# A two-layer diffusion trunk in split fp32: weight splits leave GpSimd, the last hidden group goes by token halves, one modulation block moves into the mixer

## The reference

```python
def swiglu(h, wg, wu, wd):
    return (jax.nn.silu(h @ wg) * (h @ wu)) @ wd

def ffn_sublayer(s, m, i, g, wg, wu, wd):
    h = modulate(rmsnorm(s, g), m[3 * i], m[3 * i + 1])
    return s + 0.5 * m[3 * i + 2] * swiglu(h, wg, wu, wd)

def hybrid_layer(x, ctx, mod_x, mod_c, p, lam_init, rope, need_ctx_out):
    x, ctx = ffn_sublayer(x, ...), ffn_sublayer(ctx, ...)
    h = modulate(rmsnorm(x, p['g_mix']), mx[3], mx[4])
    ...
    y = concat([a_lat, conv_lat, four_lat]) @ p['w_out']   # attention, convolution, Fourier
    x = x + mx[5] * y                                      # and the same for ctx in layer 0
    x, ctx = ffn_sublayer(x, ...), ffn_sublayer(ctx, ...)
```

## Time and profile before

| what | us |
|---|---|
| runs: median, lowest, highest | 2766.89, 2766.89, 2768.28 |
| profiled execution, and its span | 2764.62, 2762.8 |
| TensorE matmul busy | 2614.2 (95% of the span) |
| VectorE busy | 1979.2 (72%) |
| ScalarE busy | 958.2 (35%) |
| GpSimd busy | 197.9 (7%) |
| TensorE's mean granted clock, of full speed | 0.979 |

### The profile page before, as it was taken

One profiled execution on the slowest core, in us unless ns is written; L12 is line 12 of the kernel. 1 busy time (PEld: TensorE's weight loads), 2 busy tenths in 40 slices (PEclk: granted clock), 3 DMA queues, 4 the chain that ended last, 5 costly groups with the idle time before them and its releaser, 6 DMA issues.

```text
span 2762.8 us, 40297 instructions
## 1 busy us (share of the span) xinstructions
PE 2614.2 (95%) x14704; PEld 2368.5 (86%) x14704; DVE 1979.2 (72%) x3130; ACT 958.2 (35%) x1674; POOL 197.9 (7%) x324
## 2 busy tenths in 40 slices
PE   6999999979987999999998999999999988899998
PEld 4899999968955879999998799999988846788886
DVE  5688888888837377888887877777758665544445
ACT  4333333323147333332332434333423264322222
POOL 2000000030003210000001100000020013100001
PEclk8999999989999999999999999999999999999999
DMA  8134333331101113323333133334313110222221
GB/s 297 54 109 132 117 100 106 119 110 61 64 31 46 31 54 93 118 93 125 106 115 117 44 103 115 104 106 125 118 41 97 62 61 31 77 92 91 91 91 61
DMA packets 190672, 256.21 MB, mean 93 GB/s; under 512 B 7262, under 2 KB 130764, under 8 KB 190540
## 3 DMA queue, kind: packets, MB, share of 16 engines
q1 hardware_dynamic: 190540, 254.43, 29.1%
HBM read 252.31 MB, written 2.10 MB: 92 GB/s over the span
## 4 chain that ended last, share of the span: by engine, by line
PE 84%; DVE 8%; ACT 3%; issue 2%; DMA 1%; POOL 1%; DVEq 0%; ACTq 0%; SPq 0%; POOLq 0%
PE ps L1182 26%; PE ps L1184 25%; PE ps L1183 25%; PE ps L1628 1%; PE ps L1652 1%; PE ps L1573 1%; DVE h_lo L2241 1%; DVE nb L2862 1%; PE ps L1640 1%; DVE tn L2230 1%; DVE rstd L2220 1%; ACT e L2095 1%; POOL sqsum L1174 1%; DVE w_lo L2214 1%; DMA raw<-in_w_ffn_down 1%
## 5 line engine op out<-in xcount | busy, mean ns | idle before, releaser
L1182 PE MATMUL ps<-h_hi,w_hi 128*128 128x384 f32 (+2 forms) x2440 | 845.0, 346 | 26.8 <-DVE h_lo L2241 18.5
L1184 PE MATMUL ps<-h_hi,w_lo 128*128 128x384 f32 (+2 forms) x2440 | 838.9, 344 | 0.0
L1183 PE MATMUL ps<-h_lo,w_hi 128*128 128x384 f32 (+2 forms) x2328 | 802.8, 345 | 0.0
L1182 PEld LDWEIGHTS ps<-h_hi,w_hi 128*128 128x128 f32 x2440 | 465.3, 191 | 69.8 <-issue 23.4
L1184 PEld LDWEIGHTS ps<-h_hi,w_lo 128*128 128x128 f32 x2440 | 465.1, 191 | 31.8
L1183 PEld LDWEIGHTS ps<-h_lo,w_hi 128*128 128x128 f32 x2328 | 444.1, 191 | 30.6 <-issue 1.5
L1731 ACT ACTIVATE w_hi<-raw 128x512 fp32r<-128x512 f32 x348 | 210.1, 626 | 351.1 <-PE ps L1184 271.9
L1182 PE MATMUL ps<-t_hi,w_hi 128*128 128x384 f32 x864 | 294.3, 341 | 0.0
L1184 PE MATMUL ps<-t_hi,w_lo 128*128 128x384 f32 x864 | 293.6, 340 | 0.0
L1183 PE MATMUL ps<-t_lo,w_hi 128*128 128x384 f32 x864 | 293.4, 340 | 0.0
L2302 DVE SCALAR_TENSOR_TENSOR side_acc<-side_raw,ccol,side_acc 128x512 f32<-128x512 f32 x364 | 257.9, 744 | 4.2 <-DMA side_raw<-in_w_ada 3.9
(11 more groups left out here) (210 smaller groups left out, 3660.6 us busy)
## 6 DMA issues: line engine op xcount, KB each, us to landing
side_raw<-in_w_ada SPq DMA_DIRECT2D x240, 256.0 KB, 2.7
raw<-in_w_ffn_gate SPq DMA_DIRECT2D x44, 1024.0 KB, 5.3
raw<-in_w_ffn_up SPq DMA_DIRECT2D x44, 1024.0 KB, 5.3
raw<-in_w_ffn_down SPq DMA_DIRECT2D x44, 1024.0 KB, 5.0
raw<-in_w_in SPq DMA_DIRECT2D x14, 1024.0 KB, 5.3
ada_buf<-in_w_ada SPq DMA_DIRECT2D x12, 1024.0 KB, 12.6
raw<-in_w_out SPq DMA_DIRECT2D x8, 1024.0 KB, 5.2
raw<-in_w_in SPq DMA_DIRECT2D x8, 512.0 KB, 7.1
```

Source lines behind the costliest of these rows:

```text
L1182: mm(out, wh, xh, start=start, stop=False, skip_group_check=reopened)
L1183: mm(out, wh, xl, start=False, stop=False, skip_group_check=reopened)
L1184: return mm(out, wl, xh, start=False, stop=stop, skip_group_check=reopened)
```

## The change

It has five parts.

- GpSimd splits no weight tile; `POOL_SPLITS` is gone and VectorE does those eight. At the end of an FFN of `FAST` ScalarE and VectorE split the first of the next two tiles ahead of the last group's product, and the second after two residual adds of the second piece. At the end of a mixer VectorE splits `U` behind its last residual add.
- The last group's hidden tile is finished by token halves: the right half (`right_slots`, ScalarE's high half, `hid_low_half(x, 1)`), for which the down product's first piece waits, then the left (`left_slots`, `hid_low_half(x, 0)`), for which the second piece waits.
- The side product of group 9 comes after the fifth of the last seven products (`LAST_EVENT = 4`), and shift and scale of the next norm are made ahead of the last product, not between the residual adds and the reciprocal.
- The modulation block of group 10 in FFN 0 (block 16 of layer 0) moves into the first mixer: its loads behind a small table's, its sixteen sums behind the convolution taps, its side product behind the first attention scores.
- The first piece's `stat` comes after the second tile (j == 1) of the second piece at the ends of FFNs 0 to 2. The second piece's comes after the second k step of the first up product (all gate products ahead of it) in FFNs 1 to 3, and at k == 3 in the mixer's projection.

```diff
-FIRST_EVENT, SECOND_EVENT, LAST_EVENT = 4, 4, 1
+FIRST_EVENT, SECOND_EVENT, LAST_EVENT = 4, 4, 4
+MIX_SIDE = (0, NG - 1)
+STAT_AT = (None, 1, 1, 1)
...
-POOL_SPLITS = {1: (("K", 0, 0), ("K", 0, 1)), 2: (("U", 1, 0),), 3: (("G", 2, 0), ("U", 2, 0)),
-               4: (("K", 1, 0), ("K", 1, 1)), 5: (("U", 3, 0),)}
...
@@ the sync engine's queue, mixer @@
+                if key == ("S", 0):
+                    side(*MIX_SIDE, range(KD))
...
@@ GpSimd @@
-                for key in POOL_SPLITS.get(q, ()):
-                    if q % 3 != 2:
-                        split(key)
                 for s, j in square_order(q):
-                    if q % 3 == 2 and (s, j) == (seg_order(q)[1], 6):
-                        for key in POOL_SPLITS[q]:
-                            split(key)
...
@@ TensorE @@
-                                if k == 2 and s == first and ws == "g" and q:
+                                if k == STAT_AT[f] and s == first and ws == "u":
                                     stat(q, second)
...
-                pe.wait_ge(hid_ready, hid_number(f, g))
                 first, second = last_slots(f)
                 for s in (first, second):
                     o, n = PIECES[s][:2]
+                    pe.wait_ge(hid_ready, hid_number(f, g, 0 if f in FAST and s == first else 1))
...
-                        if s == second and j == 3:
+                        if s == second and j == (1 if f in FAST else 3):
                             stat(after, seg_order(after)[0])
-                    if s == first:
-                        side(lambda x: x, NG - 1)
...
-                        if s == 1 and k == 2:
+                        if s == 1 and k == 3:
                             stat(q, 0)
...
+                    if (l, i) == (0, 0):
+                        side_product(MIX_SIDE[0], lambda x: x, MIX_SIDE[1])
...
@@ ScalarE @@
                 for j in range(KD):
                     square(q, first, j)
+                if f in FAST:
+                    split(nxt[1])
+                    for j in range(2):
+                        square(q, second, j)
+                    root(q, first)
...
@@ VectorE @@
                         middle("U", x)
-                        side_end(q)
-                        side(x, (0, 1))
-                        corner("U", x)
-                        side(x, (2, 3))
-                        first_block(x)
-                        right_block(x)
-                        side(x, (4, 5))
-                        lower_blocks(x)
-                        hid_low(x)
-                        side(x, (6, 7))
+                        corner("U", x)
+                        if SIDE_GROUPS[f]:
+                            dve.wait_ge(side_done, side_number((f, p)) + 1)
+                        shift_scale((1, 3, 4)[f] // 3, (1, 3, 4)[f] % 3)
+                        split(nxt[0])
+                        first_block(x)
+                        right_slots(x)
+                        side_end(q)
+                        hid_low_half(x, 1)
+                        left_slots(x)
+                        hid_low_half(x, 0)
                         return
...
+                if f in FAST:
+                    for j in range(2):
+                        add_one(j, second)
+                    split(nxt[1])
+                    add_one(2, second)
+                    last_seg = second
+                    first, second = seg_order(q)
+                    over_rms(q, first)
...
+                if l == MIX_SIDE[0]:
+                    side_rows(*MIX_SIDE, range(KD))
...
                     add_out(2 * v + 1, s)
+                    if (v, s) == (3, second):
+                        split(("U", 2 * l + 1, 0))
```

192 lines of the change are left out of this document (107 added, 85 removed).

## The result

The changed kernel takes 2736.81 us (median of four runs, 2733.11 to 2741.49), the kernel before 2766.89 us (four runs, 2765.81 to 2768.28). The ratio is 0.9886, with a 95% interval from 0.9873 to 0.9899: 30 us less. The forecast was 2726, with a range from 2717 to 2740. The profiled execution took 2733.11 us with a span of 2731.3, so 31.5 us less than that of before.

A forecast was written before the change was run, and what follows sets the result against it. TensorE was taken as the bound, losing time only in waits and lower clock at five seams; gains of 41.6 us less 0.6 gave 41 us off the profiled 2764.62, 2723.6, plus 2.3 for the median: 2726, range 2717 to 2740.

The forecast's parts named there:

- (a): Rival: VectorE becomes the bound at the seams through held reciprocals and late GpSimd additions; 10 to 13 us return, 2737; chance 0.15.
- (b): Rival: the gain at the second and third FFN's starts is lost again as VectorE bounds their first groups; 2733; chance 0.11.
- One sign that the prediction had named for being wrong: New TensorE waits inside the FFNs' first groups; the other sign was waits for VectorE growing by more than 10 us.
- The held VectorE instruction: At the seams between sublayers, a GpSimd split of 4.60 us holds VectorE about 4.06 us; VectorE's own split takes 2.28.
- 8 x (4.06 - 2.28) = 14 us: VectorE's gain from taking back eight GpSimd splits, each said to hold it 4.06 us against 2.28 for its own.
- Seam 1: First FFN's end to first mixer: the mixer's second piece starts at 609.9 instead of 624.57, 14.7 us gained.
- Seams 2 and 5: Ends of the first and second mixer, into the second and last FFN: 5.6 and 10.1 us gained.
- Seam 3: Second FFN's end to third FFN: the second piece starts at 1541.2 instead of 1551.16, 10.0 us gained.
- Seam 4: Third FFN's end to second mixer: only the token halves and the order act, 1.2 us gained.
- less 0.6 for the second pieces at seams 2 and 3: Deduction of 0.6 us at the second and third FFN's starts, where second pieces follow VectorE's low halves step by step.
- unpriced by any row: A reciprocal beside a GpSimd addition: taken as 0, or held up to 1.3 us at each of three seams.
- (c): Rival: the side block's loads and sums in the mixer delay VectorE's mean subtraction; slower than before, 2774; chance 0.03.

The follow-up runs named there:

- pool_back: The changed kernel with the eight weight splits on GpSimd again: 2741.47 us, ratio 0.9911 to the kernel before.
- before_dve_splits: The kernel before with only the eight weight splits moved from GpSimd to VectorE: 2760.65 us, ratio 0.9979 to the kernel before.
- stat_bank_j2: stat_bank with the first piece's sum of squares asked for after the second piece's third tile at the ends of FFNs 0 to 2: 2726.98 us.
- best_a: stat_bank with the second piece's sum of squares asked for earlier, during the first gate products, in FFNs 1 and 2: 2726.59 us, ratio 0.9854.
- stat_old: The changed kernel with the sums of squares over the partitions asked for in their old places: 2744.16 us, ratio 0.9910 to the kernel before.
- stat_bank: The changed kernel with the second piece's sum of squares in the PSUM bank that the ninth product will use: 2730.09 us, ratio 0.9868.
- second execution: The changed kernel itself profiled once more, nothing altered; its second set of runs had a median of 2739.30 us.
- halves_off: The changed kernel with the last group's product, high and low halves made whole again, not by token halves: 2740.49 us, ratio 0.9895.

## Why the prediction was right, and where it was not

**Forecast and result.** Faster was right, and the time lay within the range, though near its upper end: 2736.81 us in the first set of runs and 2739.30 in the second, where the range ends at 2740. The gain was 30 us by the medians and 31.5 in the profiled executions, against 41. The range had room for this loss because of rivals (a) and (b), and neither of them was its cause. One sign that the prediction had named for being wrong did come: new waits inside the FFNs' first groups, of 1.10, 1.07 and 2.28 us.

**The held VectorE instruction** was read rightly: 4.56 us beside GpSimd's split, 0.56 without. The choice of this row against the notion that offloading helps a busy VectorE is borne out by pool_back (5 us slower) and before_dve_splits (6 us faster than before). The two pages quoted there don't stand against each other, either: the Trainium skill ("Perfetto Trace Analysis", section "Optimizing Scalar/DVE Operations") goes on in its next sentence that GpSimd and VectorE share an SBUF read port, so that moving work between them might not help. But "8 x (4.06 - 2.28) = 14 us" was too much. Only five of the eight splits held a VectorE instruction, since the residual adds beside the other three read PSUM: the row for it was in the trace. The other three only add their 2.28 us to VectorE, so in VectorE's time the price is 5 x 4.06 less 8 x 2.28, which is 2 us. The 14 us were no term of the forecast's sum, which went seam by seam; there the runs show 6 us for the splits moved alone, and steps of 7 us when they are put back.

**Seam 1.** "The down product starts at 573.3": 572.69. "587.5" for the reciprocal: 586.50. "22.4" from there to the second piece's first low half: 608.06 + 0.75 - 586.50 = 22.3. The wait before the down product was 1.5 us, not 3.0, mostly since shift and scale took 0.26 + 0.24 us, not 0.87 + 1.38: in the rows of before, single instructions of 0.78 and 1.30 us stand beside GpSimd's additions, where they take 0.17 otherwise. Behind this short wait the clock stayed up (1.00 from 572 to 610 us), and the eight tiles took 5.9 us, not the 7.4 that the forecast had for a partly lower clock. "The sum of squares, asked for two tiles earlier, isn't late" was wrong: TensorE waited for it for 1.64, 1.65 and 1.72 us at seams 1, 3 and 4. stat_bank_j2 shows that this cost nothing, because VectorE sets the end of these seams.

**Seams 2 and 5** came out as the forecast had them, 5.6 for 5.6 and 10.0 for 10.1.

**Seam 3: the step that failed there** was "the third FFN's sum of squares in its later place is asked for before VectorE is through the first piece, and costs nothing". VectorE was through earlier and idle for 4.24 us, and the seam gave 7.3 us instead of 10.0; asked for earlier, in best_a, it gives 1.3 us of that back. Seam 4 gave 3.4 instead of 1.2; stat_old shows 3.2 us there for the later sum in the projection, which the forecast had priced at nothing.

**The step that made the sum too large** was "less 0.6 for the second pieces at seams 2 and 3, which now follow VectorE's low halves step by step". This term measured 2.6 at each of the two, and 4.9 at seam 5. The short stops themselves are there (48 matmuls take 11.25 us instead of 10.68, so 0.6 in each second piece); the rest is the bank that the moved sum of squares takes, with ScalarE's split and table load in front of the silu that frees it, and the lower clock behind the longest of the waits. I had followed each engine's queue past the moved instruction, but not the rotation of the banks.

**Rival (b)**, the gain that doesn't last, was right in place at two seams and not far off in size (7.4 us at the two, where 5.2 were lost, and 4.9 more at a third), and wrong in cause: stat_bank takes the loss away without touching VectorE.

**Rival (a)** failed for the reciprocals: 1.74 us beside GpSimd's additions at seams 1, 3 and 4, and 1.75 without one. The forecast called this price "unpriced by any row", but its own row of 603.67, 1.75 us, stands beside the end of a GpSimd addition. It was right that a split holds a GpSimd addition at every seam (2.36 us for 1.28 at seams 1, 3 and 4, 2.60 for 1.26 at seam 2, 2.25 for 0.74 at seam 5), but not that this makes the seams late: the second piece's start came as forecast or earlier at all but seam 3, where the sum of squares was asked for too late. **Rival (c)**: the side block cost nothing. Four sums and their loads took about 4.4 us a pair (4.2 forecast), and VectorE had 5.1 us to spare behind them. The 1.7 us lost in the first mixer are clock: the granted clock was 0.50 from 801 to 806 us and 1.00 at the same place in the second execution, which lost as much near 768 instead; halves_off, with the same side block in its mixer, lost nothing there against the kernel before. What the move is worth against sums in the new order, 14 us, was not forecast at all.

## What to carry to other kernels

When an instruction moves, follow what it holds as well as the queues: here one PSUM bank taken two products later turned a quarter of the seams' gain into waits on another engine's silu, and a table of banks written beside the order would have shown it. An engine that blocks another while it runs should work where the other is idle: the same split cost 8 us more over three seams ahead of two residual adds than behind them. And when several parts are changed together, measure them by taking one out of the whole: here they sum to some 44 us by the medians where the whole gave 30, probably since each relies on the others to keep VectorE's queue free.
